# Latent feed-forward gate and up columns by seven block products per slot, in a two-block model kernel on one Trainium2 core

## The reference

```python
FFN_HIDDEN = ((8 * D_MODEL + 3 * 256 - 1) // (3 * 256)) * 256    # 2816

def swiglu(u, w_ffn_in, w_ffn_out):
    a, b = jnp.split(u @ w_ffn_in, 2, axis=-1)
    return (jax.nn.silu(a) * b) @ w_ffn_out

x = layer_norm(DEEPNORM_ALPHA * x + g2 * swiglu(modulate(x, sh2, sc2), w_ffn_in[l], w_ffn_out[l]), ln2_g[l], ln2_b[l])
```

## Time and profile before

| | |
|---|---|
| median of 3 runs | 2203.15 us |
| span of the profiled execution | 2203.0 us |
| PE busy | 1987.3 us, 90% |
| DVE / ACT / POOL busy | 588.5 / 423.4 / 206.2 us |
| feed-forward columns, layer 0, to the first of the way back | 1557.88 to 1700.37 us |
| the same, layer 1 | 1968.99 to 2108.19 us |

### The profile page before, as it was taken

One profiled execution on the slowest core, in us unless ns is written; L12 is line 12 of the kernel. 1 busy time (PEld: TensorE's weight loads), 2 busy tenths in 40 slices (PEclk: granted clock), 3 DMA queues, 4 the chain that ended last, 5 costly groups with the idle time before them and its releaser, 6 DMA issues.

```text
span 2203.0 us, 32618 instructions
## 1 busy us (share of the span) xinstructions
PE 1987.3 (90%) x14122; PEld 1389.8 (63%) x14122; DVE 588.5 (27%) x1120; ACT 423.4 (19%) x778; POOL 206.2 (9%) x183
## 2 busy tenths in 40 slices
PE   8999899887888888887898887999999999999997
PEld 3857575643455556653565543756888876588886
DVE  6766310124212000000002103353432044640001
ACT  2222221222202000000001212444200032630001
POOL 0730000020000000000000000334000002700000
PEclk9999999999999999999999998999999999999999
DMA  9958899999999999999999998531686743044450
GB/s 365 372 199 343 339 420 424 417 427 426 421 426 427 423 418 426 420 425 426 421 425 426 416 423 343 140 116 39 222 294 199 180 144 116 1 153 153 129 158 20
DMA packets 181383, 664.24 MB, mean 302 GB/s; under 512 B 17432, under 2 KB 121401, under 8 KB 142649
## 3 DMA queue, kind: packets, MB, share of 16 engines
q1 hardware_dynamic: 181240, 662.16, 76.7%
HBM read 661.08 MB, written 1.05 MB: 301 GB/s over the span
## 4 chain that ended last, share of the span: by engine, by line
PE 58%; DMA 30%; DVE 5%; ACT 4%; issue 1%; POOL 1%; SPq 1%; ACTq 0%; DVEq 0%; POOLq 0%
PE ps L1213 19%; PE ps L692 11%; DMA ring<-in_w_up 8%; DMA ring<-in_w_gate 7%; DMA ring<-in_w_down_slots 7%; DMA ring<-in_context_weights 6%; PE ps L1663 5%; PE ps L1689 2%; PE ps L1048 2%; PE ps L1012 2%; PE ps L1323 2%; DMA arena<-in_w_ada 2%; PE ps L1222 2%; PE ps L1568 1%; ACT arena L2605 1%
## 5 line engine op out<-in xcount | busy, mean ns | idle before, releaser
L1213 PE MATMUL ps<-arena,ring 128*128 128x256 f32 x1984 | 429.9, 379 | 1.0 <-DVEq L392 0.9
L1213 PEld LDWEIGHTS ps<-arena,ring 128*128 128x128 f32 x1984 | 376.5, 190 | 54.2 <-issue 1.7
L1663 PE MATMUL ps<-ring,arena 128*32 128x256 f32 x4000 | 260.5, 407 | 76.2 <-DMA ring<-in_w_up 43.4
L692 PE MATMUL ps<-arena,ring 128*128 128x256 f32 (+1 forms) x1392 | 319.2, 390 | 6.5 <-DMA ring<-in_context_weights 6.5
L692 PEld LDWEIGHTS ps<-arena,ring 128*128 128x128 f32 (+1 forms) x1392 | 256.0, 190 | 76.3 <-DMA ring<-in_context_weights 23.4
L1663 PEld LDWEIGHTS ps<-ring,arena 128*32 128x32 f32 x4000 | 125.4, 115 | 194.9 <-DMA ring<-in_w_up 59.4
L2311 ACT ACTIVATE arena<-ps 128x512 f32<-128x512 f32 (+4 forms) x147 | 78.2, 532 | 739.7 <-PE ps L692 326.8
L1689 PE MATMUL ps<-ring,arena 128*32 128x512 f32 x1024 | 136.9, 660 | 54.4 <-DMA ring<-in_w_down_slots 50.6
L1689 PEld LDWEIGHTS ps<-ring,arena 128*32 128x32 f32 x1024 | 29.0, 114 | 141.1 <-DMA ring<-in_w_down_slots 87.0
L3116 POOL TENSOR_TENSOR XC<-XC,arena 128x256 f32<-128x256 f32 x32 | 23.4, 730 | 986.0 <-ACT XC L2406 965.7
L692 PE MATMUL ps<-ring,arena 128*128 128x256 f32 (+3 forms) x320 | 87.6, 425 | 0.0
(11 more groups left out here) (387 smaller groups left out, 1982.6 us busy)
## 6 DMA issues: line engine op xcount, KB each, us to landing
ring<-in_w_down_slots SPq DMA_DIRECT2D x64, 2048.0 KB, 14.5
ring<-in_w_up SPq DMA_DIRECT2D x63, 2048.0 KB, 13.6
ring<-in_w_gate SPq DMA_DIRECT2D x62, 2048.0 KB, 14.1
ring<-in_w_ada SPq DMA_DIRECT2D x27, 2048.0 KB, 9.6
ring<-in_w_ffn_in SPq DMA_DIRECT2D x44, 1024.0 KB, 7.7
ring<-in_context_weights SPq DMA_DIRECT2D x35, 1024.0 KB, 14.7
ring<-in_w_ffn_out SPq DMA_DIRECT2D x16, 1408.0 KB, 7.4
ring<-in_w_in SPq DMA_DIRECT2D x9, 2048.0 KB, 11.6
```

Source lines behind the costliest of these rows:

```text
L692: m = mm(o, a, x, start=(k == 0 and r == 0), stop=(k == kt - 1 and last))
L1213: m = mm(b, w[:, k, c:c + P], src[:, k, :], start=(k == 0), stop=(k == kt - 1))
L1663: m = mm(b[u][32 * c:32 * c + 32, T * x:T * x + T], xs[:, 2 * h + k, CAP * e:CAP * e + CAP], w[:, k, at_:at_ + T], start=(h == 0 and k == ...
```

## The change

For slots 1 to 10 of both latent layers the product of one slot, 256 tokens x 1024 x 512 columns, is cut in halves of tokens, contraction and columns, and its eight block products are replaced by seven with sums of blocks (Winograd's form). A block product is four matmuls: tokens (or token sums) are stationary, 256 weight columns move. So the output is by token, not by column.

- Token sums `S1` to `S4`, four VectorE instructions a layer. Weight sums: `T3` (in the ring, in place) and `T2` on VectorE, `T1` and `T4` on GpSimd, in every slot.
- ScalarE copies the first product out of PSUM; VectorE joins the seven products in six instructions, ScalarE takes SiLU of the gates, VectorE multiplies (`hid_tok`), TensorE transposes it with four transposes, ScalarE evacuates these into `HID`.
- The slot's columns are laid out beforehand, one contiguous load in place of two.
- VectorE's work on `late_i` stands in iteration i+2 in place of i+1; the late rows of TensorE stand inside slots 6 and 10.
- Some semaphores of the first block are merged.

The blocks of a slot, and TensorE:

```diff
+            def weight_blocks(l, j):
+                w = slot(fi_slot[l, j], stream[fi_slot[l, j]][1])
+                return [[w[:, 4 * k:4 * k + 4, T * f:T * f + T] for f in range(2)] for k in range(2)]
...
                 for j in range(1, 11):
-                    w = take(f"fi{j}{N}")
-                    for x, kind in enumerate(("fa", "fb")):
-                        b = open_bank(pe, f"{kind}{j}_{N}")
-                        tile(b[:, 0:T], w, T * x, U, 2 * l + 1 if j == 1 and x == 0 else None)
-                        close_bank(tile(b[:, T:2 * T], w, T * x + P, U), f"{kind}{j}_{N}")
-                    release_with(f"fb{j}_{N}")
+                    only = j == 1
+                    take(f"fi{j}{N}")
+                    (B11, T3), (B21, B22) = weight_blocks(l, j)
+                    T1, T2, T4 = w_sum[j % 2]
+                    b = open_bank(pe, f"f1{j}_{N}")
+                    product(b[:, 0:T], U11, B11, turn=0 if only else None)
+                    pe.wait_ge(sums_made, weights_summed(l, j) - 1)
+                    if only:
+                        pe.wait_ge(sums_made, 24 * l + 3)
+                    close_bank(product(b[:, T:2 * T], S3, T3), f"f1{j}_{N}")
+                    b = open_bank(pe, f"f2{j}_{N}")
+                    product(b[:, 0:T], U12, B21, turn=4 if only else None)
+                    pe.wait_ge(sums_made, weights_summed(l, j))
+                    if only:
+                        pe.wait_ge(sums_made, 24 * l + 5)
+                    close_bank(product(b[:, T:2 * T], S2, T2), f"f2{j}_{N}")
+                    if j > 1:
+                        hidden_turned(j - 1)
+                    if l == 0 and j in (6, 10):
+                        late_rows(1 + j // 10)
+                    b = open_bank(pe, f"f3{j}_{N}")
+                    pe.wait_ge(pool_sums, 2 * order(l, j) + 1)
+                    product(b[:, T:2 * T], S1, T1)
+                    pe.wait_ge(pool_sums, 2 * order(l, j) + 2)
+                    close_bank(product(b[:, 0:T], U22, T4), f"f3{j}_{N}")
+                    b = open_bank(pe, f"f4{j}_{N}")
...
+                    close_bank(product(b[:, 0:T], S4, B22), f"f4{j}_{N}")
+                    release_with(f"f4{j}_{N}")
```

VectorE:

```diff
                 centre(X, l, 0)
+                weight_sums(l, 1)
                 normed(X, l, 0)
...
                 for j in range(1, 11):
+                    n = order(l, j)
+                    dve.wait_ge(p1_copied, n + 1)
+                    b2, b1 = read_bank(dve, f"f2{j}_{N}"), read_bank(dve, f"f1{j}_{N}")
+                    step(tt(with_sixth, first_copy, b2[:, T:2 * T], ALU.add))
+                    step(tt(with_seventh, with_sixth, b1[:, T:2 * T], ALU.add), frees=f"f1{j}_{N}")
+                    step(tt(blocks[:, 0, :], first_copy, b2[:, 0:T], ALU.add), frees=f"f2{j}_{N}")
+                    if j < 10:
+                        weight_sums(l, j + 1)
+                    b3 = read_bank(dve, f"f3{j}_{N}")
+                    step(tt(blocks[:, 1:4:2, :], bc(with_seventh, 1, 2, T), b3[:].rearrange("p (i t) -> p i t", i=2), ALU.add), blocks_made)
+                    step(tt(with_sixth, with_sixth, b3[:, T:2 * T], ALU.add), frees=f"f3{j}_{N}")
+                    b4 = read_bank(dve, f"f4{j}_{N}")
+                    step(tt(blocks[:, 2, :], with_sixth, b4[:, 0:T], ALU.add), frees=f"f4{j}_{N}")
                     dve.wait_ge(sga_ready[X], 11 * l + j + 1)
...
+                    step(tt(hid_tok, sga[:, j % 2, :].rearrange("p (i t) -> p i t", i=2), blocks[:, 2:4, :], ALU.mult), blocks_made)
...
-                    if l == 0 and j < 9:
-                        late_slot(j - 1)
+                    if l == 0 and 2 <= j < 10:
+                        late_half(j - 2, 0)
+                        late_half(j - 2, 1)
```

GpSimd:

```diff
+                for j in range(1, 11):
+                    _, (B21, B22) = weight_blocks(l, j)
+                    T1, T2, T4 = w_sum[j % 2]
+                    pool.wait_ge(sums_made, weights_summed(l, j))
+                    step(nc.gpsimd.tensor_tensor(T1, B22, T2, ALU.subtract), pool_sums)
+                    step(nc.gpsimd.tensor_tensor(T4, B21, T2, ALU.subtract), pool_sums)
```

More of the change, by code:

```diff
@@ L619, in build, with order, weights_summed @@
             top += size
+        fi_slot = {(l, j): n for l in range(2) for j in range(11) for n, (name, _) in enumerate(stream) if name == f"fi{j}x{l}"}
+        def order(l, j):
+            return 10 * l + j - 1
+        def weights_summed(l, j):
+            return 24 * l + (2 if j == 1 else 2 * j + 4)
+        def weight_blocks(l, j):
+            w = slot(fi_slot[l, j], stream[fi_slot[l, j]][1])
+            return [[w[:, 4 * k:4 * k + 4, T * f:T * f + T] for f in range(2)] for k in range(2)]
         def slot(n, src):
@@ L1238, in latent, with product @@
                 release_with(f"rb1{N}")
-                for j in range(1, 11):
-                    w = take(f"fi{j}{N}")
-                    for x, kind in enumerate(("fa", "fb")):
-                        b = open_bank(pe, f"{kind}{j}_{N}")
-                        tile(b[:, 0:T], w, T * x, U, 2 * l + 1 if j == 1 and x == 0 else None)
-                        close_bank(tile(b[:, T:2 * T], w, T * x + P, U), f"{kind}{j}_{N}")
-                    release_with(f"fb{j}_{N}")
+                def product(o, tokens_, weights, turn=None):
+                    for k in range(4):
+                        if turn is not None:
+                            pe.wait_ge(u_ready[X], KD * (2 * l + 1) + turn + k + 1)
+                        m = mm(o, tokens_[:, k, :], weights[:, k, :], start=(k == 0), stop=(k == 3))
+                    return m
@@ new lines, in hidden_turned @@
+                def hidden_turned(j):
+                    pe.wait_ge(blocks_made, 2 * order(l, j) + 2)
+                    b = open_bank(pe, f"fh{j}_{N}")
+                    for i in range(2):
+                        for t in range(2):
+                            m = tr(b[:, T * i + P * t:T * i + P * t + P], hid_tok[:, t, P * i:P * i + P], ident)
+                    close_bank(m, f"fh{j}_{N}")
+                (U11, U12), (U21, U22) = [[U[:, 4 * k:4 * k + 4, P * t:P * t + P] for k in range(2)] for t in range(2)]
@@ L2086, in dve_mixers @@
             step(stt(out=ab, in0=fi, scalar=-1.0, in1=fi, op0=ALU.mult, op1=ALU.max))
-            tell(g_ready)
+            tell(g_steps)
             dve.wait_ge(g_ln, 1)
-            step(stt(out=LF, in0=FI, scalar=0.0, in1=LG, op0=ALU.min, op1=ALU.subtract), lf_ready)
+            step(stt(out=LF, in0=FI, scalar=0.0, in1=LG, op0=ALU.min, op1=ALU.subtract), g_steps)
             qk_conv(0)
@@ L2144, in dve_mixers @@
             qk_conv(1)
-            tell(conv_ready)
+            tell(g_steps)
             dve.wait_ge(hc_ready, 3)
@@ L2231, in dve_moe @@
             step(tt(aff, logit, bc(rsm, 2, TT, NE), ALU.mult))
-            tell(aff_ready)
+            tell(sel_steps)
             ada()
@@ L2821, in raw_hidden, with weight_sums @@
                     tell(raw_gate)
+            def weight_sums(l, j):
+                n = fi_slot[l, j]
+                (B11, B12), (B21, B22) = weight_blocks(l, j)
+                T2 = w_sum[j % 2][1]
+                dve.wait_ge(landed[n % LANES], landing[n])
+                step(tt(B12, B22, B12, ALU.subtract), sums_made)
+                step(tt(T2, B12, B11, ALU.add), sums_made)
+            def raw_hidden(l, N):
                 for i in range(2):
```

173 lines of the change are left out of this document (104 added, 69 removed).

## The result

The changed kernel takes 2268.05 us (median of 4 runs, 2265.36 to 2272.55), the kernel before 2201.28 beside it: ratio 1.0303, 95% interval 1.0286 to 1.0320. It is slower by 66.8 us where 56.9 was forecast against the 2203.15 of that time (2260; range 2224 to 2272). The profiled execution's span is 2270.8 us, 67.8 above the one before.

The account below looks back on a forecast made before the run. TensorE, busy 90%, was taken to bound the kernel before; in layer 0 a loop through ring DMA and VectorE would then set the slots. Layer 0 +68.7 and layer 1 -11.6 gave +57.1 on 2203.15: 2260 us, range 2224 to 2272.

Parts of the forecast that it names:

- The loop: Layer 0, slots 4 to 9: weights' landing, VectorE's sums and late work, next DMA issue; 25.1 us a turn.
- The port: VectorE's two-SBUF-input instructions wait out GpSimd's T1 and T4; layer 0 period 25.1 us, 22.2 if nothing is blocked.
- rivals 1 and 2: Layer 0 loop with port wait, 2260 us, 50%; loop with port wait mostly absent, 2235 (to 2245), 27%.
- The products: TensorE's latent slots: 28 matmuls for 32, plus four transposes; 12.65 us a slot, 1.16 less than 13.8.
- The sum for layer 1: Layer 1's ten slots 126.5 us plus 1.1 at the start, against 139.2 before: 11.6 us gained.
- The start's loss at S3: Block start: sums run beside the norm, and TensorE loses about 1.1 us waiting at S3.
- the sum: Whole kernel: layer 0 +68.7 us, layer 1 -11.6, net +57.1, giving 2260 us.
- fi10, issued alone: Layer 0's last weight load, issued after late6's use, lands 7.6 us after issue.
- slot 10: Layer 0's last slot: 12.65 us plus 1.0 for late rows, which wait 5.1 more for late7's use.
- From layer 0's way back to layer 1's slots: Last transposes, 0.55 us, and the late turn, 0.95, move into this stretch.
- TensorE's clock: After idling, about 3.4 us at the lower clock, costing 1.7 us of work per resumption; changes nothing in the total.
- Rival 3: Layer 0 loop with TensorE at its low clock level through the slots: 2275 us, 7%.

Follow-up runs that it names:

- Experiments 1 and 2: Changed kernel, late pieces one slot later in the stream: 2195.42 us; changed kernel, VectorE's late_i work back in iteration i+1, stream unchanged: 2199.27 us.
- experiment 4: Kernel before, with VectorE's late work one iteration later and TensorE's late rows and turns moved along, nothing else of the change: 2220.47 us.
- experiment 7: Changed kernel, with VectorE's weight sums in layer 0 placed behind the hidden product and late work: 2252.96 us.
- Experiment 3: Changed kernel without GpSimd's sums T1 and T4, TensorE using T2 for both, so output is not the reference's: 2243.32 us.
- experiment 5: Changed kernel with late pieces one slot later in the stream and late rows at the ends of slots 6 and 10: 2184.12 us.

## Why the prediction was right

**The loop.** Right in kind, place and size. Landing to landing was forecast as 25.1 us, 124.4 for the five from slot 4 to slot 9; measured 124.6. Of a turn DMA was to take 12.5 (12.3 to 12.55 in five of six, 13.4 in one) and VectorE 12.6 (12.3 in the one read above). Experiments 1 and 2 take the relation of late piece and use away from either end and recover 73 and 69 us; experiment 4 shows that the later use costs 20 without the seven products, and experiment 7 that with the sums behind the late work TensorE no longer waits for the ring.

**The port.** 25.1 against 22.2 was the choice between rivals 1 and 2. Experiment 3 decides for the first: 22.8 on average without GpSimd's sums for 24.9 with them, and VectorE's part of a turn 9.7 to 10.0 for 12.3. The Trainium skill ("SBUF — State Buffer", section "SBUF: two separate sides") calls it an exclusive lock for a whole instruction; the trace agrees, also for the long instructions: T4 takes 2.68 beside the hidden product that got in first, 2.35 alone, and the modulation step behind T4 pays about 2 (4.34 for 2.35). VectorE's three additions that read PSUM run beside T1 at their usual 0.69, 0.42 and 0.42.

**The products.** The sum for layer 1 was 126.5 + 1.1 = 127.6; measured 127.7. That it meets to 0.1 us is luck. A slot takes 12.5 us in this layer, forecast 12.65: four transposes inside other work cost 0.44 us (1592.49 to 1592.93), less than the 0.55 of the earlier trace rows. The start's loss at S3 was forecast as 1.1, measured 0.89. What these leave over is taken up by a wait of 1.45 us in slot 2, which stood in no term.

**What the sum missed: 10 us.** In layer 0 the block took 214.2, forecast 209.7. The 4.5 us have three main parts.

The first is a port wait that I left out. Slot 2 waits 1.45 us for a bank of the raw products (those of `fi0`), which VectorE frees at L2919, behind slot 1's additions. I counted the port in the norm and in the loop, but not here. VectorE and GpSimd's T4:

```profile
1573.89 1.94 DVE L2891 TENSOR_TENSOR arena<-arena 128x256 f32<-128x256 f32 x1
1575.87 0.49 DVE L2919 SCALAR_TENSOR_TENSOR arena<-arena,ps 128x256 f32<-128x256 f32 x1
```

```profile
1572.87 2.68 POOL L3245 TENSOR_TENSOR arena<-ring,arena 128x1024 f32<-128x1024 f32 x1
```

The product with two inputs in SBUF ends behind T4 (1575.55) and takes 1.94 for 0.42, and the hidden product ahead of it 1.27 for 0.69: 2.1 us together, more than the 1.45. In experiment 3, without GpSimd's sums, the two take 0.42 and 0.69, and TensorE doesn't wait there at all.

The second is fi10, issued alone: it landed 8.7 us after its issue where I took 7.6, though the earlier trace rows have 7.5 to 9.6.

The third is slot 10, 20.4 us for 18.8. I named its lower clock, but put it at nothing in the sum. The clock is low twice: 7.02 for 5.34 at the start, and 5.39 for 3.62 behind the wait at the late rows (granted 0.77 from 1751.9 to 1758.8, 0.68 from 1765.4 to 1770.6). The first stretch costs nothing, since late7's sums, for which the rows wait, end at their time anyway: the wait is 3.3 us where I had 5.1. The second stretch, 1.8 us, is passed on.

From layer 0's way back to layer 1's slots it was 275.7 against 268.6: 1.5 was forecast, and the other 5.6 lie outside the change's slots. Most of it is one place in layer 1's attention:

```profile
1922.23 0.42 PE L876 MATMUL ps<-arena 32*32 32x32 f32 x31 [2.21 <-issue]
1922.58 5.28 PE L714 MATMUL ps<-arena,ring 128*128 128x256 f32 x16
```

TensorE stands 2.2 us amid a run of 32x32 instructions with nothing to wait for in the profile, and the next 16 take 5.28 where they took 3.72: 3.8 us together. Over these 16 the granted clock was 0.70, then 1.00 again. The stall is there in all variants of the changed kernel, 2.0 to 2.5 us, and not in the kernel before or in experiment 4. The changed TensorE program has another number of instructions ahead of this place. The trace also has single packets of a queue that loads instructions, though not whose: one at 1919.5 to 1919.75, just ahead of the stall, and in experiment 5 likewise (1835.25 to 1835.5, stall from 1835.8); in the kernel before they fall at 1841.25 and 1846.5, outside this run of 32x32 instructions (1844.5 to 1846.3). That TensorE waits for its instructions here would fit, but wasn't tested, and it stays open. Two more waits of 0.7 us are new in this stretch: for a bank behind VectorE's raw queries (L740 for L2897) and in the output projection (L1242 for L2863); what delays VectorE there wasn't looked into.

**TensorE's clock.** In 11 us with 1.65 busy, and in the 14 us behind them, the granted clock (the column ahead of the last two) reads:

```profile
1620.00:1631.00 11.00, 1.65 (x8) 1.12 (x6) 0.00 (x0) 0.00 (x0) 0.00 (x0) 0.75 0.90 372
1631.00:1645.00 14.00, 13.98 (x56) 11.98 (x57) 13.02 (x11) 1.61 (x3) 5.04 (x2) 0.83 0.05 8
```

Rival 3, the low level (1.2 GHz for 2.4) through whole slots, falls: it came back to full within each slot, at 1.7 to 2.9 us of TensorE's time (7.01 to 8.23 for 24 instructions that take 5.34), which the loop hid.

## What to carry to other kernels

A ring that is filled in order ties every piece to the consumer of the piece one round earlier, also a piece that another engine consumes. Whoever moves a consumer by one step has to move its piece in the stream too: here four changed lines are worth 73 us, and with the late rows at a place where their input is ready the seven-product form gains 17.6 us on the kernel before. And an engine's average load says little once it waits for a load on behalf of another: add up the whole circle, landing, sums, next release, next landing, and compare it with a slot.

## What the runs showed of the hardware that was not expected

- A stall of 2.0 to 2.5 us that no semaphore explains, with 1.6 us at the lower clock behind it, in a place whose code is the same before and after. Its cause is open.
- The time of a pair of loads, a late piece and 2 MB of weights queued right behind it, varies for the same code. From the first issue to the second landing it is 12.3 to 13.4 us in the changed kernel, 12.35 to 13.8 in experiment 3, and 13.35 to 14.8 in experiment 4, where the weights come in two loads of 1 MB. That the layout makes the difference isn't shown: the ranges overlap.
- A wait of TensorE costs more than its length: behind waits of 2.6 to 5.0 us the next slot of experiment 4 takes 1.7 us longer, and behind 5.3 to 10.3 us the next 24 instructions of the changed kernel take 1.7 to 2.9 longer, in no order with the wait's length.
